# Three token-mixing layers in fp32: products of the next weights taken up inside each layer norm, an early split of GLA's last weights, and GpSimd's passes held back

## What is computed

```python
def first_block(x, ...):
    for i in range(2):                  # i = 0: sparse attention + pooling; i = 1: gated linear attention (GLA)
        mix = nsa_pool_mixer(x, ...) if i == 0 else gla_mixer(x, ...)
        x = layer_norm(ALPHA * x + mix, ln1_g[i], ln1_b[i])                      # norms 0 and 2
        x = layer_norm(ALPHA * x + square(relu(x @ w1[i])) @ w2[i], ln2_g[i], ln2_b[i])  # norms 1 and 3

def gla_mixer(x, w_in, ...):
    q, k, v, r, a = split(x @ w_in)     # 512, 512, 1024, 1024, 16 columns
    ...
    o = o * rsqrt(mean(o * o) + eps) * norm_g
    return (o * silu(r)) @ w_out

def second_block(h, ...):
    mix = hybrid_mixer(h, ...)          # gated delta rule (8 heads) beside a spatial gating unit
    h = layer_norm_2(A2 * h + mix, ...)                                          # norm 4
    return layer_norm_2(A2 * h + hierarchical_moe(h, ...), ...)                  # norm 5, the last

def hierarchical_moe(x, ...):           # all 16 experts are computed; combine is zero for those not chosen
    h = silu(einsum("td,edf->tef", t, w_gate)) * einsum("td,edf->tef", t, w_up)  # f = 256
    h = h * combine[:, :, None]
    return einsum("tef,efd->td", h, w_down)
```

## Time and profile before

| | |
|---|---|
| median of three runs | 1382.78 us |
| profiled execution, own time | 1382.79 us |
| span of that execution | 1381.1 us |
| mean granted clock of TensorE | 0.959 |
| busy share TensorE, VectorE, ScalarE, GpSimd | 93%, 60%, 43%, 13% |
| HBM read | 202.63 MB, 147 GB/s over the span |

### The profile page before, as it was taken

The page is one execution under the profiler, slowest core; times in us unless marked ns, Lnnn a source line. Parts: engine busy times, 40 slices in busy tenths (PEclk is TensorE's granted clock), DMA queues, the critical chain, the costliest instruction groups (busy, mean ns, idle before and its releaser), DMA issues.

```text
span 1381.1 us, 20765 instructions
## 1 busy us (share of the span) xinstructions
PE 1291.1 (93%) x8982; PEld 1206.1 (87%) x8982; DVE 828.4 (60%) x972; ACT 599.0 (43%) x693; POOL 178.5 (13%) x140
## 2 busy tenths in 40 slices
PE   7998999998997799998998998899899899999996
PEld 7977899997997699997988988899799799999995
DVE  6567755556527855556596439753567655555554
ACT  4565343334644444334563347423933453333331
POOL 8301300004000400000403100120400400000002
PEclk9998999999998999999899989899999899999999
DMA  9712655554514355557785338753455345555550
GB/s 263 177 41 95 220 194 192 183 183 133 174 62 156 133 202 189 192 195 123 88 139 110 62 62 152 123 59 65 156 197 186 118 162 190 189 189 185 183 183 31
DMA packets 160220, 205.02 MB, mean 148 GB/s; under 512 B 13571, under 2 KB 142322, under 8 KB 160130
## 3 DMA queue, kind: packets, MB, share of 16 engines
q1 hardware_dynamic: 157906, 195.80, 51.0%
q0 software_dynamic: 2224, 7.90, 1.7%
HBM read 202.63 MB, written 1.05 MB: 147 GB/s over the span
## 4 chain that ended last, share of the span: by engine, by line
PE 82%; DVE 7%; ACT 5%; DMA 3%; issue 2%; POOL 1%; POOLq 0%; SPq 0%; DVEq 0%; ACTq 0%
PE PS L358 23%; PE PS L359 23%; PE PS L360 23%; DMA ring<-in_w_in 2%; DVE w_lo L971 2%; PE PS L816 2%; ACT w_hi L1534 1%; PE PS L828 1%; PE PS L824 1%; POOL AR L1994 1%; DVE AR L1311 1%; PE PS L572 1%; PE PS L594 1%; ACT AR L1564 1%; PE PS L494 1%
## 5 line engine op out<-in xcount | busy, mean ns | idle before, releaser
L971 DVE TENSOR_TENSOR w_lo<-ring,w_hi 128x2048 fp32r<-128x2048 f32 x182 | 435.2, 2395 | 253.4 <-ACT w_hi L1534 253.2
L358 PE MATMUL PS<-x_hi,w_hi 128*128 128x256 f32 x1696 | 499.1, 294 | 30.4 <-DVE x_lo L1015 13.1
L359 PE MATMUL PS<-x_lo,w_hi 128*128 128x256 f32 x1696 | 490.0, 289 | 0.0
L360 PE MATMUL PS<-x_hi,w_lo 128*128 128x256 f32 x1696 | 489.7, 289 | 0.0
L1534 ACT ACTIVATE w_hi<-ring 128x2048 fp32r<-128x2048 f32 x182 | 347.2, 1911 | 285.3 <-PE PS L360 268.2
L358 PEld LDWEIGHTS PS<-x_hi,w_hi 128*128 128x128 f32 x1696 | 336.6, 198 | 38.0 <-issue 18.4
L359 PEld LDWEIGHTS PS<-x_lo,w_hi 128*128 128x128 f32 x1696 | 336.2, 198 | 3.3 <-issue 1.7
L360 PEld LDWEIGHTS PS<-x_hi,w_lo 128*128 128x128 f32 x1696 | 335.6, 198 | 0.0
L1546 ACT ACTIVATE AR<-PS 128x512 f32<-128x512 f32 (+1 forms) x145 | 82.9, 586 | 326.3 <-PE PS L360 210.3
L358 PE MATMUL PS<-w_hi,o_hi 128*128 128x512 f32 x480 | 188.5, 393 | 3.6 <-DVE o_lo L1182 3.6
L359 PE MATMUL PS<-w_lo,o_hi 128*128 128x512 f32 x480 | 187.4, 390 | 0.0
(11 more groups left out here) (368 smaller groups left out, 1396.4 us busy)
## 6 DMA issues: line engine op xcount, KB each, us to landing
ring<-in_mlp_w SPq DMA_DIRECT2D x64, 1024.0 KB, 5.2
ring<-in_w_in SPq DMA_DIRECT2D x32, 1024.0 KB, 9.8
ring<-in_expert_w_gate SPq DMA_DIRECT2D x16, 1024.0 KB, 5.4
ring<-in_expert_w_up SPq DMA_DIRECT2D x16, 1024.0 KB, 5.4
ring<-in_expert_w_down SPq DMA_DIRECT2D x16, 1024.0 KB, 4.9
ring<-in_c_w_in SPq DMA_DIRECT2D x12, 1024.0 KB, 5.4
ring<-in_a_w_in SPq DMA_DIRECT2D x4, 1024.0 KB, 9.3
ring<-in_c_w_out SPq DMA_DIRECT2D x4, 1024.0 KB, 5.0
```

The costliest lines, as they stand in the source:

```text
L358: mm(out, a_hi, b_hi, start=first, stop=False, skip_group_check=True)
L359: mm(out, a_hi, b_lo, start=False, stop=False, skip_group_check=True)
L360: return mm(out, a_lo, b_hi, start=False, stop=last, skip_group_check=True)
L971: v.tensor_tensor(w_lo[:, m % PARTS], ring[:, index[split[m]] % RING], w_hi[:, m % PARTS].bitcast(F32), ALU.subtract)\
```

## The change

It has four parts.

**1. The next chunk's first token tile during the norm.** `last_rows` now begins, behind its own last product, the chunk named by `then` by token, in bank 0: two steps (k = 0, 1 of token tile 0), then the transposes of token tile 1; the other 14 steps follow. `then` is f0w1 0, gv 0, f1w1 0, uv 4 and eg 0 for norms 0 to 4. Its waits are for the first two low halves in token tile 0 and the last two in token tile 1. ScalarE does both high halves of tile 0 ahead of tile 1's deviation.

The diff, cut to its core:

```diff
+        cols("gv", cwi, 1024, 1)
         cols("gq", cwi, 0, 2)
         cols("gk", cwi, 512, 2)
-        cols("gv", cwi, 1024, 4)
+        cols("gv", cwi, 1024 + W, 3, 1)
...
             def triples(chunk, bank, token=False, layer=None):
...
-                        if m == 0 and k % 4 == 0 and layer is not None:
-                            pe.wait_ge(S("x_split"), 4 * (layer + 1) + 3 + k // 4)
+                        if k % 4 == 0 and layer is not None:
+                            pe.wait_ge(S("x_split"), 4 * (layer + 1) + 2 * m + k // 4 + 1)
...
-            def last_rows(chunks, k0, pre, ready, ln=None):
+            def last_rows(chunks, k0, pre, ready, ln=None, then=None):
...
                 if ln is not None:
+                    steps = triples(then, 0, True, ln)
+                    advance(steps, 2)
                     norm_transposes(ln, 1)
+                    return steps
+
+            def turned(src, pre):
+                ps = claim(pe, pre, nxt(4, 8))
+                for m in range(2):
+                    for t in range(TT):
+                        ins = nc.tensor.transpose(ps[:, m * T + t * P:m * T + (t + 1) * P], src[:, t * T + m * P:t * T + (m + 1) * P], ident[:])
+                close(ins, pre)
...
-            def feed_forward(l, ln):
-                for c in range(NFF):
-                    by_feature((f"f{l}w1", c), lo=4, hi=8, layer=ln if c == 0 else None)
+            def feed_forward(l, ln, steps, then):
+                advance(steps)
+                for c in range(1, NFF):
+                    if c == 1:
+                        steps = triples((f"f{l}w1", 1), nxt(4, 8))
+                        advance(steps, 8)
+                        read_out(pe, (f"f{l}w1", 0))
+                        turned(f_h[:, 3], ("fT", l))
+                        advance(steps)
+                    else:
+                        by_feature((f"f{l}w1", c), lo=4, hi=8)
...
-                    fill = in_turn([(("gs", i), False) for i in range(4)] + [(("uv", i), True) for i in range(4, 8)])
+                    fill = in_turn([(("gs", i), False) for i in range(4)] + [(("uv", i), True) for i in range(5, 8)])
...
+            steps = triples(("eu", 0), 1)
+            advance(steps, 8)
+            read_out(pe, ("eg", 0))
+            turned(flat(e_sg[:, 1]), "egT")
+            advance(steps)
...
                     high_half(l, 0, 0)
+                    high_half(l, 0, 1)
                 deviation(1)
                 n_norm[0] += 1
                 if not last:
-                    high_half(l, 0, 1)
                     high_half(l, 1, 0)
...
+            split_ahead(pieces_for[("gr", 1)], PARTS)
             for h in range(4):
...
+            pool.wait_ge(S("hidden"), 2)
             affine(0, 0)
...
+            affine(1, 1)
+            pool.wait_ge(S("hidden"), NFF + 2)
+            affine(2, 2)
+            affine(3, 3)
...
+            pool.wait_ge(S("expert_h"), 2)
             affine(5, 4)
```

More of the change, by code:

```diff
@@ L360, in products, with by_feature @@
                 return mm(out, a_lo, b_hi, start=False, stop=last, skip_group_check=True)
-            def by_feature(chunk, a_hi=x_hi, a_lo=x_lo, lo=0, hi=8, ready=None, layer=None, halves=None):
+            def by_feature(chunk, a_hi=x_hi, a_lo=x_lo, lo=0, hi=8, ready=None, halves=None):
                 if halves is not None:
@@ L383, in triples @@
             def triples(chunk, bank, token=False, layer=None):
+                assert token or layer is None
                 n = take(chunk)
@@ L665, in _ @@
                 close(ins, ("gb", t))
-            for i in range(4):
+            for i in range(1, 4):
                 by_token(("gv", i))
```

75 lines of the change are left out of this document (47 added, 28 removed).

## The result

The changed kernel took 1342.74 us, the median of four runs (1338.9 to 1347.48), against 1382.1 for the kernel before beside it: a ratio of 0.9711 with a 95% interval of 0.9682 to 0.9739. That is 39.4 us less, and outside the forecast, 1355.5 with a range of 1347 to 1368, on the better side. Six more runs of the same kernel, taken later beside other experiments, had a median of 1350.8 and a ratio of 0.9770 (0.9738 to 0.9802). The median of all ten is 1346.3 (1338.9 to 1354.1), that of 75 executions of the kernel before, taken beside all of these and the experiments, 1382.0. So the gain is nearer 35.7 than 39.4.

A forecast was written before the change was run, and what follows sets the result against it. TensorE, busy 93% of the span, was taken to bound the kernel through its work, gaps and half clock. Gains of 32.5 us (clock held) or 21.3 (fallen) gave a middle of 27: 1355.5 us, range 1347 to 1368.

The forecast's parts named there:

- The norm, one after the other: At each norm, next-chunk products fill TensorE's idle time: chunk end 15.05 to 10.05 us, 5.0 gained if the clock holds.
- clock held everywhere: All five norms and GLA with TensorE's clock staying up: the terms sum to 32.5 us gained.
- my fallen case: Clock falls behind every norm as before: chunk ends at 12.9, 2.2 us gained a norm, 21.3 in all.
- Holding GpSimd: Feed-forwards behind norms 0 and 2: GpSimd's passes held back, TensorE's waits for o_lo of 1.57 and 2.03 go, 3.6 us.
- GLA's split: In GLA, VectorE splits gr 3 and gout 0 earlier: 7.1 us wait and 2.5 of half clock go, 9.6 us.
- Norm 1: Norm ahead of GLA, tile used as it stands: 5.0 less a w_lo wait of 0.7, 4.3 us, or 2.1 fallen.
- Norm 4: Norm ahead of the experts, tile turned: 4.3 us gained, or 1.6 fallen; the experts' new order worth nothing.
- Norm 3: Norm ahead of the hybrid mixer, uv chunk moved out of head block 1's fill: net 2.5 us, or 1.0, down to 0.
- the held passes cost where they land: Rival: under the loops of chunks, a debt of 3 us is paid in each of three holds; 1365 us, chance 0.07.
- the token tile does nothing: Rival: at the norms the early products gain nothing, only GLA's 7 to 10 and two stalls remain; 1370 us, chance 0.04.
- the slower case: Rival: VectorE has no slack under the holds, 26 us lost, and turned tiles come late, another 8; 1390 us, chance 0.02.
- the first rival: At the norms the clock isn't held and added waits reach 1 to 2 us each; 1362 to 1369 us, chance 0.14.

The follow-up runs named there:

- a_ctrl: The changed kernel again with the same code, six later executions as the yardstick for other runs: median 1350.8 us, ratio 0.9770 to the kernel before.
- a_warm: The changed kernel with 16 more transposes of the identity on TensorE behind the last product of each norm: median 1346.0 us, ratio 0.9722.

## Why the prediction was wrong, step by step

**The norm, one after the other: right.** All dates of norm 0's chunk lie within 0.3 us of the forecast, its end 10.3 for 10.05.

**The clock: the step that failed.** "I take the middle, 27". Measured are 35.7, against 32.5 for clock held everywhere. Between held and fallen lay 11.2 us, and the forecast credited half of them; that is 5.5 of the 8.7 us by which it fell short. (Taken from 1382.78 the middle is 1355.8, not 1355.5.) I had argued from the row where the clock fell, although there two idle stretches of 3 us come close together, which the change does away with. The windows show 1.00 or 0.89, for 0.66 and 0.77 before. It fell in seven of ten, but for 3.4 us in place of 6.8 to 10.2, and such a fall costs 0.7 to 0.9 us a norm, not the 2.8 that my fallen case assumed. That case, a chunk end at 12.9, never occurred: the latest in the changed kernel's two profiles is 11.2. With the held sum the forecast would have been 1350.3, inside the executions of the changed kernel but still above the median of its ten. That the held terms without hold and split, 19.3, are what was measured for the token tile by the medians is in part luck: norms 1 and 2 gave less than their terms and norms 3 and 4 more, as the table shows. The sign "The forecast is wrong if the clock falls in all norms" was set too strictly as well: in a_ctrl it fell in all five, and most of the gain was there.

**The spread: missing from the range.** Two sets of executions of the changed kernel have medians of 1342.7 and 1350.8. The range began at 1347 and took in unknown costs, but not the 4 us or so by which the median of a few executions differs from that of ten (1342.7 and 1350.8 against 1346.3). The median of ten is within 1 us of the range's end, the forecast's centre 9 off.

**Holding GpSimd: alone right, its role under-told.** 3.6 was forecast and 3.2 measured alone. "That fits only without GpSimd" was said and not priced: with the token tile the holds are worth 15 to 19 us. The debts that I feared under the loops (3 us a hold) don't show: no product waits there.

**GLA's split: right.** 9.6 forecast, 8.8 to 9.9 measured alone.

**Norm 1: over-priced.** 4.3 against 1.7 to 2.2. Of the difference, 0.8 is a wait of gout 0 for ScalarE, which stands in the changed kernel with and without the early split and in no kernel without the token tile. The clock at 0.89 in its window (up to 0.9) and w_lo (0.3) may be part of the rest, but no run shows it: the stretch took 124.1 us in a_warm with the clock held, and 124.0 in a_ctrl.

**Norm 4: under-priced** by 2. Before, the clock also fell a second time in the chunks behind the router's sums, for 6.8 us, which I left at its price though the trace had it; it is 3.4 now. That this makes up the 2 us is not shown.

**Norm 3: the sign right, the size not settled.** The rotation of banks was in no term: moving a chunk out of an order renumbers who shares a bank with whom.

**The rivals.** That the held passes cost where they land, that the token tile does nothing, and the slower case all fell. So did the first rival, a gain of 14 to 21 us. Its ground was half right: the clock falls anyway behind most norms, but too briefly to cost what it did, and the waits that were to grow stayed at 0.3 for w_lo behind a norm.

## What to carry to other kernels

Work that is moved onto a short chain must find its helpers free: the same GpSimd passes cost 15 to 19 us, nearly all of it in two feed-forwards, and nothing that shows 10 us later. Price a possible fall of the clock from the idle stretches that the changed order leaves, not from the stretch that it fell in before, and then ask whether TensorE or another engine's chain sets the end there; only in the first case is the clock worth its price. And before two kernels are compared by 5 us, look how far ten executions of one of them differ.

## What the runs showed of the hardware

Executions of one kernel differed by 15 us (ten of the changed one) and 18 us (71 of the one before), in step with the time that TensorE spent at 1.2 GHz (0.41 us for each). Sixteen transposes of a 128x128 constant took 1.91 us at full clock, and with them behind the last product the granted clock was 1.00 for 14 us behind all five norms (a_warm); behind norm 4 it fell after that. A cast of 128x512 on VectorE went from 0.43 to 2.51 us beside a GpSimd pass, and the square, cast and subtraction of a hidden result from 1.8 to 6.5 us. One idle stretch of 2.4 or 3.5 us was followed by 3.4 us at 1.2 GHz or none behind a norm; two of 3.05 and 2.2 to 2.9 us with eight transposes between them by 6.8 to 10.2.
